# Late half of the first prompt block's index scores in the sample's top-k list, and the index key and head weights in one pass of 72 columns

## The chip, the cores and the metric

The kernel runs on one core of a Trainium2 chip, in one launch. The metric is the device time of that execution in microseconds, the median of several runs. TensorE (PE), VectorE (DVE), ScalarE (ACT), GpSimd (POOL) and SyncE (SP, which issues most DMAs) each run their own instruction stream, in order, and meet only at semaphores.

## The reference

A streaming encoder step of two layers for 256 prompt frames and 32 sample frames of width 1024, all in float32. Each layer is a half-step FFN, a mixer, and a second half-step FFN, each with RMS norms. The mixer's input projection `w_in` has columns for a convolution branch (a, g), attention (q, k, v, 8 heads of 64) and an indexer (8 index queries of 64, one shared index key of 64, 8 head weights). The indexer decides which keys each query may attend to:

```python
logits = jnp.einsum('thd,sd->ths', qi, ki).astype(jnp.float32) * IDX_SCALE
score = jnp.einsum('th,ths->ts', wi.astype(jnp.float32) * IDX_HEAD_SCALE, jax.nn.relu(logits))
admissible = k_chunk[None, :] <= q_chunk[:, None]
score = jnp.where(admissible, score, -jnp.inf)
_, idx = lax.top_k(score, topk)
valid = k_chunk[idx] <= q_chunk[:, None]
```

A chunk has 64 frames, and a query sees the keys of its own chunk and of earlier ones. A prompt query keeps the top 64 of 256 keys; a sample query the top 136 of 544 (512 cached ones and 32 new). The first 64 prompt queries have exactly 64 admissible keys, so they keep all of them; queries 64 to 127 choose 64 of 128, and those from 128 on choose from 192 or 256. Softmax attention over the kept keys, a causal convolution of width 31 with layer norm and swish beside it, and one output projection follow.

## The kernel before

Activations lie transposed, channels in the 128 partitions and the 288 tokens along the row. Every float32 weight is split into a high and a low part: ACT copies it to `whi` (L403), VectorE (L712) or, in the mixers, GpSimd (L1050) subtracts to `wlo`, and three matmuls (L1110 to L1112) multiply wlo by hh, whi by hl and whi by hh. A projection unit is 128 output columns: 24 matmuls. SP streams the weights through two raw slots; a slot's next load waits for the low splits that read it. The order of work is written out by hand for each engine.

The mixer's stages on TensorE: step 0 of the input projection (units 0 to 3, the index queries, `first_step`); then the index key and the head weights, called the tail; then the partner products of the rotation (L1221, one for each of the four index-query tiles and one for kiT) between the units of step 1. Partner k from 2 on waits for rotation k-2 to be done (`rope_done`), since two PSUM banks serve five products. Then come the transposes of head weights and cached keys, the index logits of eight heads, steps 2 to 5 of the projection (in the code `in_step`), the partners of q and k, value transposes, and ten attention rounds (`logits`, `turn`, `values`). `partners(9)` waits until the rotations of q are done.

The tail's weights come in by three DMAs from GpSimd's queue (L1083): the 64 key columns twice, so that the key lands in both halves of the partitions, and the 8 head-weight columns; 136 columns in all. ACT splits the high part (L492), VectorE the low part (L876). TensorE makes two passes of 24 matmuls (L1207 to L1209), one with 128 columns to bank 4 and one with 8 columns to bank 5, and ACT copies them to kiT (L505) and wiT (L507).

VectorE in the mixer: L876; the reciprocal root (L727); cosR and sinR (L879, L880); the rotations (L838 multiplies a tile by cosR, L839 the partner in PSUM by sinR, L843 adds them); the head weights (L884 to L896); then for each head two operations that add a weighted relu'd logit tile to the score tile (L903, L905): 128 columns for prompt queries 0 to 127, 256 for queries 128 to 255. Two memsets of 64 x 64 bar the inadmissible keys (L910, L911), L913 copies the sample's scores (32 rows, 544 columns) behind them, and `top_k` runs. A round of a list is one MAX8 (L864: the eight largest of each row) and one MATCH_REPLACE8 (L866: mark these as taken), each waiting for the one before on the same list. Two lists are interleaved: the sample's with 17 rounds of 32 x 544, and the prompt's with eight rounds of 128 x 128 followed by eight of 128 x 256.

```python
top_k([[(slice(0, DEC), 384, 928, TOPK_S)],
       [(slice(0, P), 0, P, TOPK_P), (slice(0, P), P, 384, TOPK_P)]])
```

After that VectorE scales the conv branch by the inverse root (L922, L923; the first releases ACT's sigmoid, L537, and through it ACT's copies and weight splits of step 4), makes the sample's mask in four copies (L926) and the prompt's in place over 384 columns (L928), multiplies the gate (L933, L934, which release ACT's and its own convolution work), runs 8 of its 83 convolution steps (L946, L950), rotates q, runs 14 more steps, rotates k, and goes on with convolution steps between the attention rounds. GpSimd splits weights (L1050, four operations a step), each released by ACT's high split, and later adds convolution products (L1097).

Of the kernel before, what the change touches and what calls it, by code (L numbers as in the profile page):

```python
# [15 lines left out]
ALU = mybir.AluOpType  # L16
ACT = mybir.ActivationFunctionType

P = 128
D = 1024  # L20
SEQ = 256
DEC = 32
T = SEQ + DEC
# [27 lines left out]
WIDX = 2 * HD + HEADS  # L51
# [38 lines left out]
def build(nc, ins, consts, outs):  # L90
    (y_prompt, y_sample, prompt_k, prompt_v, prompt_ki, prompt_conv,
     sample_k, sample_v, sample_ki, sample_conv) = outs
    with ExitStack() as ctx:
# [5 lines left out]
        def sb(name, shape, dt=F32):  # L99
            size = int(np.prod(shape[1:])) * 4  # L100
            t = nc.alloc_sbuf_tensor_at(name, list(shape), dt, offset=BASE + at[0])
            at[0] += (size + 31) // 32 * 32
            assert at[0] <= SIZE - 64, (name, at[0])
            return t
# [39 lines left out]
        wiT = sb("wiT", [HEADS, T])  # L144
# [6 lines left out]
        score = sb("score", [P, 928])  # L151
# [9 lines left out]
        wtlo = sb("wtlo", [P, KD, WIDX], F32R)  # L161
        rel_at = at[0]
# [227 lines left out]
        def _(act):  # L390
# [97 lines left out]
            def mixer(m, s):  # L488
                u = mix_unit(m)

                act.wait_ge(tail_in, 48 * (m + 1))
# [12 lines left out]
                act.wait_ge(tail_done, 2 * m + 1)  # L504
                act.activation(kiT[:], bank(4), ACT.Copy).then_inc(tail_saved, 1)  # L505
                act.wait_ge(tail_done, 2 * m + 2)
                act.activation(wiT[:], bank(5, slice(0, HEADS)), ACT.Copy).then_inc(tail_saved, 1)  # L507
# [192 lines left out]
        def _(dve):  # L700
# [172 lines left out]
            def mixer(m, s, g, hq_next, g_next):  # L873
# [23 lines left out]
                for h in range(HEADS):  # L897
                    dve.wait_ge(rel_ready, 8 * m + h + 1)
                    for a, b, w0 in ((0, P, 0), (P, 384, 8)):
                        src = relP[:, h % 2, a:b]  # L900
                        w = wrow[:, w0 + h:w0 + h + 1]
                        if h == 0:
                            last = dve.tensor_scalar(score[:, a:b], src, w, None, ALU.mult)  # L903
                        else:
                            last = dve.scalar_tensor_tensor(out=score[:, a:b], in0=src, scalar=w,  # L905
                                                            in1=score[:, a:b], op0=ALU.mult, op1=ALU.add)
                    last.then_inc(rel_used, 1)
                    dve.wait_ge(rel_used, 8 * m + h + 1)

                dve.memset(score[0:CHUNK, CHUNK:P], BARRED)  # L910
# [4 lines left out]
                top_k([[(slice(0, DEC), 384, 928, TOPK_S)],  # L915
                       [(slice(0, P), 0, P, TOPK_P), (slice(0, P), P, 384, TOPK_P)]])
# [11 lines left out]
                link(dve.tensor_scalar(score[:, 0:384], score[:, 0:384], TAKEN, NEG, ALU.not_equal, ALU.mult))  # L928
# [30 lines left out]
                def softmax_max(n):  # L959

                    dve.wait_ge(s_done, 10 * m + n + 1)
                    if n >= 2:
                        dve.wait_ge(pT_done, 10 * m + n - 1)
                    spans = [(0, SKEYS)] if n < 2 else [(0, P), (P, 384)]
                    c = 8 * n
                    for j, (a, b) in enumerate(spans):
                        logits = ps[:, 1024 * (n % 2) + a:1024 * (n % 2) + b]
                        mask = maskS[:] if n < 2 else score[:, a:b]
                        link(dve.tensor_tensor_reduce(prob[:, n % 2, a:b], logits, mask, HD ** -0.5, -3.0e38,  # L969
                                                      ALU.add, ALU.max, stat[:, c + j:c + j + 1]))  # L970
                    k = len(spans)
                    dve.tensor_scalar(stat[:, c + 2:c + 2 + k], stat[:, c:c + k], -1.0, None,
                                      ALU.mult).then_inc(max_ready, 1)
# [49 lines left out]

            dve.memset(ones[:], 1.0)
# [21 lines left out]
        def _(pool):  # L1046
# [29 lines left out]
            for m in range(DEPTH):  # L1076
# [4 lines left out]
                for d, (c0, n) in ((0, (KI_COL, HD)), (HD, (KI_COL, HD)), (2 * HD, (KI_COL + HD, HEADS))):  # L1081
                    with nc.allow_non_contiguous_dma(reason="8 head-weight columns"):
                        pool.dma_start(wtail[:, :, d:d + n], w_in[:, :, c0:c0 + n]).then_inc(tail_in, 16)  # L1083
# [23 lines left out]
        def _(pe):  # L1107
# [91 lines left out]
            def mixer(m, s, hq):  # L1199
# [4 lines left out]
                for b, c0, n in ((4, 0, P), (5, P, HEADS)):  # L1204
                    for k in range(KD):
                        o = bank(b, slice(0, n))
                        pe.matmul(o, wtlo[:, k, c0:c0 + n], hh[:, k, :], start=(k == 0), stop=False)  # L1207
                        pe.matmul(o, wthi[:, k, c0:c0 + n], hl[:, k, :], start=False, stop=False)
                        last = pe.matmul(o, wthi[:, k, c0:c0 + n], hh[:, k, :], start=False, stop=(k == KD - 1))  # L1209
                    last.then_inc(tail_done, 1)  # L1210
# [32 lines left out]
                for tt, (t0, n) in enumerate(TOK):  # L1243
                    pe.transpose(bank(4, slice(0, n), 8 * tt, 8), wiT[:, t0:t0 + n], ident[0:HEADS, 0:HEADS])
                    last = pe.matmul(bank(4, slice(0, n), 24 + tt, 1), rinv[0:1, t0:t0 + n], ones[0:1, 0:1],
                                     start=True, stop=True)
# [297 lines left out]
```

## Time and profile before

| | |
|---|---|
| runs | 1392.57, 1393.87, 1399.64 us; median 1393.87 |
| profiled execution | span 1389.6 us from the first to the last instruction; no own run time is listed for it |
| PE, PEld busy | 1266.4 us (91%), 1202.5 us (87%) |
| DVE busy | 936.1 us (67%), 1555 instructions |
| ACT, POOL busy | 655.4 us (47%), 290.0 us (21%) |
| mean granted TensorE clock | 0.941 |
| mixers | about 242 to 476 us and 920 to 1154 us of the span |

The busy shares are means over the FFNs, where TensorE is full, and the mixers, where it isn't. A matmul's traced duration (about 0.29 us) overlaps its neighbours'; the distance between their starts is what counts. A DVE operation's duration includes the time in which it has been started and is held up.

### The profile page before, as it was taken

Reading aid. Unit: us, or ns where it says so; the run is one execution under the profiler, and the core shown is the slowest. Engines: PE = TensorE matmul, PEld = TensorE weight load, DVE = VectorE, ACT = ScalarE, POOL = GpSimd, SP = SyncE. Lnnn points to the kernel's source line nnn. Section 1 sums busy time; section 2 is a strip of 40 time slices with the busy share of each in tenths; the row PEclk is TensorE's granted clock in tenths of the full one; section 3 lists DMA queues with packets and bytes.
Section 4 is the critical chain, followed back from the end, with each engine's and each line's share of the span. In section 5 each row is a group of like instructions: output and inputs, shape, how many; then the busy total and the mean of one; then the engine's idle time right before and its main releaser. Section 6 shows DMA issues by size and latency. Waiting matters only on the chain.

```text
span 1389.6 us, 24055 instructions
## 1 busy us (share of the span) xinstructions
PE 1266.4 (91%) x9033; PEld 1202.5 (87%) x9033; DVE 936.1 (67%) x1555; ACT 655.4 (47%) x1100; POOL 290.0 (21%) x214
## 2 busy tenths in 40 slices
PE   5999999999367899999989999999966689999998
PEld 4999999889255899999989999987964479999998
DVE  3766644779996676664476665466999957766543
ACT  3544444444365654444455444454335475544432
POOL 3000000546461610000020000035564425000000
PEclk9999999999757999999999999999985599999998
DMA  5454555523200435454535455553340023545451
GB/s 173 141 184 159 164 173 164 161 92 125 87 0 1 161 122 181 151 165 156 165 119 184 154 171 164 164 190 122 106 138 1 0 70 123 173 160 180 144 167 58
DMA packets 179540, 184.63 MB, mean 133 GB/s; under 512 B 6627, under 2 KB 174827, under 8 KB 179470
## 3 DMA queue, kind: packets, MB, share of 16 engines
q1 hardware_dynamic: 178030, 181.93, 40.6%
q0 software_dynamic: 1056, 1.62, 0.5%
q8 instruction: 46, 0.75, 0.2%
q14 instruction: 24, 0.20, 0.0%
q10 hardware_dynamic: 384, 0.13, 0.0%
HBM read 179.73 MB, written 3.93 MB: 132 GB/s over the span
## 4 chain that ended last, share of the span: by engine, by line
PE 68%; DVE 25%; ACT 3%; issue 3%; DMA 0%; DVEq 0%; SPq 0%; ACTq 0%
PE ps L1110 21%; PE ps L1112 20%; PE ps L1111 20%; DVE yc L950 6%; DVE score L866 2%; DVE acc L736 2%; DVE m L864 2%; DVE x L757 2%; DVE hl L722 2%; DVE upd L749 1%; DVE prob L981 1%; DVE prob L969 1%; DVE ropb L839 1%; PE ps L1340 1%; DVE proj L843 1%
## 5 line engine op out<-in xcount | busy, mean ns | idle before, releaser
L1110 PE MATMUL ps<-hh,wlo 128*128 128x288 f32 x1920 | 575.8, 300 | 19.2 <-DVE hl L722 10.1
L1111 PE MATMUL ps<-hl,whi 128*128 128x288 f32 x1920 | 567.6, 296 | 0.0
L1112 PE MATMUL ps<-hh,whi 128*128 128x288 f32 x1920 | 565.8, 295 | 0.0
L712 DVE TENSOR_TENSOR wlo<-raw,whi 128x1024 fp32r<-128x1024 f32 (+1 forms) x269 | 320.5, 1193 | 287.0 <-ACT whi L403 283.7
L403 ACT ACTIVATE whi<-raw 128x1024 fp32r<-128x1024 f32 (+1 forms) x336 | 347.4, 1035 | 236.5 <-PE ps L1112 213.2
L1110 PEld LDWEIGHTS ps<-hh,wlo 128*128 128x128 f32 x1920 | 361.2, 188 | 27.5 <-issue 14.2
L1112 PEld LDWEIGHTS ps<-hh,whi 128*128 128x128 f32 x1920 | 362.7, 189 | 0.0
L1111 PEld LDWEIGHTS ps<-hl,whi 128*128 128x128 f32 x1920 | 361.9, 188 | 0.6
L1050 POOL TENSOR_TENSOR wlo<-raw,whi 128x1024 fp32r<-128x1024 f32 x67 | 166.3, 2499 | 492.1 <-ACT whi L403 492.0
L1110 PE MATMUL ps<-ghi,wlo 128*128 128x288 f32 x704 | 208.4, 296 | 0.0
L1111 PE MATMUL ps<-glo,whi 128*128 128x288 f32 x704 | 207.7, 295 | 0.0
L1112 PE MATMUL ps<-ghi,whi 128*128 128x288 f32 x704 | 207.0, 294 | 0.0
L1112 PEld LDWEIGHTS ps<-ghi,whi 128*128 128x128 f32 x704 | 132.6, 188 | 0.0
L1111 PEld LDWEIGHTS ps<-glo,whi 128*128 128x128 f32 x704 | 132.2, 188 | 0.0
L1110 PEld LDWEIGHTS ps<-ghi,wlo 128*128 128x128 f32 x704 | 131.9, 187 | 0.0
L950 DVE SCALAR_TENSOR_TENSOR yc<-ext,taps,yc 128x318 f32<-128x318 f32 x160 | 116.2, 794 | 0.0
L451 ACT ACTIVATE sil<-sil 128x288 f32<-128x288 f32 x88 | 38.8, 445 | 151.2 <-DVE sil L788 151.2
L1097 POOL TENSOR_TENSOR yc<-yc,prod 128x318 f32<-128x318 f32 x78 | 70.4, 903 | 63.1 <-ACT prod L554 54.2
L1083 POOL DMA_DIRECT2D wtail<-in_w_in x6 | 5.3, 895 | 274.5 <-DVE glo L794 274.5
L736 DVE TENSOR_TENSOR acc<-acc,ysq 128x288 f32<-128x288 f32 x42 | 43.4, 1034 | 27.9 <-ACT ysq L434 26.9
L801 DVE TENSOR_TENSOR gt<-ps,rinv 128x288 f32<-128x288 f32 x88 | 40.0, 455 | 21.2 <-PE ps L1112 21.1
L458 ACT ACTIVATE ghi<-gt 128x288 f32 (+1 forms) x88 | 39.1, 445 | 31.9 <-DVE gt L805 25.5
(202 smaller groups left out, 1186.5 us busy)
## 6 DMA issues: line engine op xcount, KB each, us to landing
raw<-in_ffn_w_up SPq DMA_DIRECT2D x88, 1024.0 KB, 5.1
raw<-in_ffn_w_down SPq DMA_DIRECT2D x32, 1024.0 KB, 5.1
raw<-in_w_in SPq DMA_DIRECT2D x24, 1024.0 KB, 5.2
raw<-in_ffn_w_down SPq DMA_DIRECT2D x16, 768.0 KB, 4.5
raw<-in_w_out SPq DMA_DIRECT2D x8, 1024.0 KB, 5.1
kc<-in_cache_k SPq DMA_DIRECT2D x2, 1024.0 KB, 8.1
vc<-in_cache_v SPq DMA_DIRECT2D x2, 1024.0 KB, 8.3
xrow<-in_x_prompt SPq DMA_DIRECT2D x1, 1024.0 KB, 5.4
```

What stands on the lines that cost most here:

```text
L403: act.activation(whi[:, split_slot, 0:n, :], raw[:, raw_slot, 0:n, half * P:(half + 1) * P], ACT.Copy).then_inc(hi_ready, 1)
L451: act.activation(sil[:, j * T:(j + 1) * T], sil[:, j * T:(j + 1) * T], ACT.Silu).then_inc(silu_ready, 1)
L458: act.activation(ghi[:, bass.ds((2 * i + j) * T, T)], gt[:, j * T:(j + 1) * T], ACT.Copy).then_inc(ghi_ready, 1)
L712: dve.tensor_tensor(wlo[:, split_slot, 0:n, :], raw[:, raw_slot, 0:n, cols], whi[:, split_slot, 0:n, :].bitcast(F32), ALU.subtract).then_i ...
L736: dve.tensor_tensor(acc[:], acc[:], ysq[:, slot * T:(slot + 1) * T], ALU.add).then_inc(acc_ready, 1)
L801: dve.tensor_tensor(gt[:, j * T:(j + 1) * T], bank(b0[2 + j]), rinv[:], ALU.mult).then_inc(up_ready, 1)
L950: ins_ = dve.scalar_tensor_tensor(out=yc[:, ct, :], in0=src, scalar=w, in1=yc[:, ct, :], op0=ALU.mult, op1=ALU.add)
L1050: pool.tensor_tensor(wlo[:, split_slot, :, :], raw[:, raw_slot, :, cols], whi[:, split_slot, :, :].bitcast(F32), ALU.subtract).then_inc(lo ...
L1097: pool.tensor_tensor(dst, dst, prod[:, n % 3, :], ALU.add).then_inc(pconv_ready, 1)
L1110: pe.matmul(out, wlo[:, slot, k, :], hi, start=start, stop=False)
L1111: pe.matmul(out, whi[:, slot, k, :], lo, start=False, stop=False)
L1112: return pe.matmul(out, whi[:, slot, k, :], hi, start=False, stop=stop)
```

## The change

The head weights and the key are computed in one pass. The tail's weights are loaded once as 72 neighbouring columns by one DMA, split once (576 elements a row instead of 1,088), and 24 matmuls of 72 columns give bank 4 rows 0 to 63 (key) and 64 to 71 (head weights). ACT copies the key twice, to both halves of kiT, and the weights to rows 64 to 71 of wiT; the transposes read from there.

The scores of queries 64 to 127 go to rows 64 to 127 of the sample's area (columns 384 to 511), so that one list covers both: eight rounds over 128 rows and 544 columns, then nine over the sample's 32 rows. The rest of that area is barred by two larger memsets. Queries 0 to 63 take no part, and their mask is constant: a new tile `seen`, set up once, holds 0 for the 64 admissible keys and the mask value for the others; its rows 64 to 127 are written each layer. The prompt's other list has only the eight rounds of 256 columns. The prompt mask (L928) becomes two operations.

```diff
-WIDX = 2 * HD + HEADS
+WIDX = HD + HEADS
...
-                act.wait_ge(tail_done, 2 * m + 1)
-                act.activation(kiT[:], bank(4), ACT.Copy).then_inc(tail_saved, 1)
-                act.wait_ge(tail_done, 2 * m + 2)
-                act.activation(wiT[:], bank(5, slice(0, HEADS)), ACT.Copy).then_inc(tail_saved, 1)
+                act.wait_ge(tail_done, m + 1)
+                for half in range(2):
+                    last = act.activation(kiT[half * HD:(half + 1) * HD, :], bank(4, slice(0, HD)), ACT.Copy)
+                last.then_inc(tail_saved, 1)
+                act.activation(wiT[HD:WIDX, :], bank(4, slice(HD, WIDX)), ACT.Copy).then_inc(tail_saved, 1)
...
-                    for a, b, w0 in ((0, P, 0), (P, 384, 8)):
-                        src = relP[:, h % 2, a:b]
-                        w = wrow[:, w0 + h:w0 + h + 1]
+                    late = slice(CHUNK, P)
+                    for rows, a, b, o, w0 in ((late, 0, P, 384, 0), (slice(0, P), P, 384, P, 8)):
+                        src = relP[rows, h % 2, a:b]
+                        w = wrow[rows, w0 + h:w0 + h + 1]
+                        dst = score[rows, o:o + b - a]
...
-                dve.memset(score[0:CHUNK, CHUNK:P], BARRED)
+                dve.memset(score[late, 384 + P:928], BARRED)
+                dve.memset(score[DEC:CHUNK, 384:928], BARRED)
                 dve.memset(score[0:CHUNK, P + 3 * CHUNK:P + 4 * CHUNK], BARRED)
...
-                top_k([[(slice(0, DEC), 384, 928, TOPK_S)],
-                       [(slice(0, P), 0, P, TOPK_P), (slice(0, P), P, 384, TOPK_P)]])
+                top_k([[(slice(0, P), 384, 928, TOPK_P), (slice(0, DEC), 384, 928, TOPK_S - TOPK_P)],
+                       [(slice(0, P), P, 384, TOPK_P)]])
...
-                link(dve.tensor_scalar(score[:, 0:384], score[:, 0:384], TAKEN, NEG, ALU.not_equal, ALU.mult))
+                dve.tensor_scalar(seen[late, :], score[late, 384:384 + P], TAKEN, NEG, ALU.not_equal, ALU.mult)
+                link(dve.tensor_scalar(score[:, P:384], score[:, P:384], TAKEN, NEG, ALU.not_equal, ALU.mult))
...
-                        mask = maskS[:] if n < 2 else score[:, a:b]
+                        mask = maskS[:] if n < 2 else score[:, a:b] if a else seen[:]
...
+            dve.memset(seen[0:CHUNK, 0:CHUNK], 0.0)
+            dve.memset(seen[0:CHUNK, CHUNK:P], NEG)
...
-                for d, (c0, n) in ((0, (KI_COL, HD)), (HD, (KI_COL, HD)), (2 * HD, (KI_COL + HD, HEADS))):
-                    with nc.allow_non_contiguous_dma(reason="8 head-weight columns"):
-                        pool.dma_start(wtail[:, :, d:d + n], w_in[:, :, c0:c0 + n]).then_inc(tail_in, 16)
+                pool.dma_start(wtail[:], w_in[:, :, KI_COL:KI_COL + WIDX]).then_inc(tail_in, 16)
...
-                for b, c0, n in ((4, 0, P), (5, P, HEADS)):
-                    for k in range(KD):
-                        o = bank(b, slice(0, n))
-                        pe.matmul(o, wtlo[:, k, c0:c0 + n], hh[:, k, :], start=(k == 0), stop=False)
-                        pe.matmul(o, wthi[:, k, c0:c0 + n], hl[:, k, :], start=False, stop=False)
-                        last = pe.matmul(o, wthi[:, k, c0:c0 + n], hh[:, k, :], start=False, stop=(k == KD - 1))
-                    last.then_inc(tail_done, 1)
+                for k in range(KD):
+                    o = bank(4, slice(0, WIDX))
+                    pe.matmul(o, wtlo[:, k, :], hh[:, k, :], start=(k == 0), stop=False)
+                    pe.matmul(o, wthi[:, k, :], hl[:, k, :], start=False, stop=False)
+                    last = pe.matmul(o, wthi[:, k, :], hh[:, k, :], start=False, stop=(k == KD - 1))
+                last.then_inc(tail_done, 1)
```

## Rows read from the trace of the kernel before

**Rows 1.** The page, part 4: shares of the chain that ended last, by line
```profile
PE ps L1110 21%; PE ps L1112 20%; PE ps L1111 20%; DVE yc L950 6%; DVE score L866 2%; DVE acc L736 2%; DVE m L864 2%; DVE x L757 2%; DVE hl L722 2%; DVE upd L749 1%; DVE prob L981 1%; DVE prob L969 1%; DVE ropb L839 1%; PE ps L1340 1%; DVE proj L843 1%
```

**Rows 2.** Busy time by stretch: us, DVE busy, PEclk, DMA share, GB/s
```profile
298.70:331.00 32.30, 32.20 (x101) 1.00 0.42 130
331.00:363.00 32.00, 31.87 (x30) 0.84 0.40 132
```

**Rows 3.** Timeline of DVE, top-k of the first layer: start us, us, engine, line, operation
```profile
298.76 0.91 DVE L864 MAX8 m<-score 32x8 f32<-32x544 f32 x2
...
312.96 1.03 DVE L864 MAX8 m<-score 32x8 f32<-32x544 f32 x2
...
329.29 0.70 DVE L864 MAX8 m<-score 32x8 f32<-32x544 f32 x1
...
330.84 1.36 DVE L922 TENSOR_TENSOR proj<-proj,rinv 128x1152 f32<-128x1152 f32 x1
```

**Rows 4.** Timeline of DVE, the two clears ahead of the top-k
```profile
297.96 0.11 DVE L910 MEMSET score<- 64x64 f32 x1
298.04 0.11 DVE L911 MEMSET score<- 64x64 f32 x1
```

**Rows 5.** Groups of DVE instructions by line and form: busy us, mean ns
```profile
L731 DVE MEMSET acc<- 128x288 f32 x6 | 1.8, 298 | 0.1
```

**Rows 6.** Timeline of DVE, masks, gates, convolution and rotation of q, first layer
```profile
333.38 1.77 DVE L926 TENSOR_SCALAR maskS<-score 32x544 f32<-32x544 f32 x4
335.17 2.43 DVE L928 TENSOR_SCALAR score<-score 128x384 f32<-128x384 f32 x1
...
340.86 2.49 DVE L934 TENSOR_TENSOR ext<-proj 128x128 f32<-128x128 f32 x1
...
346.43 10.82 DVE L950 SCALAR_TENSOR_TENSOR yc<-ext,taps,yc 128x318 f32<-128x318 f32 x5
...
358.20 0.45 DVE L839 TENSOR_TENSOR ropb<-ps,sinR 128x288 f32<-128x288 f32 x1
```

**Rows 7.** Timeline of POOL in the first mixer, with idle time before and its releaser
```profile
265.12 2.59 POOL L1050 TENSOR_TENSOR wlo<-raw,whi 128x1024 fp32r<-128x1024 f32 x1
...
272.29 2.48 POOL L1050 TENSOR_TENSOR wlo<-raw,whi 128x1024 fp32r<-128x1024 f32 x1 [4.59 <-ACT whi L403]
...
334.72 10.89 POOL L1050 TENSOR_TENSOR wlo<-raw,whi 128x1024 fp32r<-128x1024 f32 x4 [8.44 <-ACT whi L403]
346.81 10.09 POOL L1050 TENSOR_TENSOR wlo<-raw,whi 128x1024 fp32r<-128x1024 f32 x4 [1.20 <-ACT whi L403]
356.86 2.94 POOL L1097 TENSOR_TENSOR yc<-yc,prod 128x318 f32<-128x318 f32 x3
```

**Rows 8.** Timeline of PE around the tail's two passes and the partner products
```profile
260.19 0.29 PE L1207 MATMUL ps<-hh,wtlo 128*128 128x288 f32 x1
...
266.50 1.13 PE L1221 MATMUL ps<-proj,swap 128*128 128x288 f32 x4
...
270.66 0.65 PE L1221 MATMUL ps<-proj,swap 128*128 128x288 f32 x2
...
272.68 0.72 PE L1221 MATMUL ps<-proj,swap 128*128 128x288 f32 x2 [1.37 <-DVE proj L843]
```

**Rows 9.** Timeline of DVE, sinR and rotation of the index queries, first layer
```profile
262.82 2.65 DVE L880 TENSOR_TENSOR sinR<-sinT,rinv 128x288 f32<-128x288 f32 x1
267.25 0.77 DVE L838 TENSOR_TENSOR ropa<-proj,cosR 128x288 f32<-128x288 f32 x1 [1.78 <-PE ps L1221]
...
272.09 0.45 DVE L843 TENSOR_TENSOR proj<-ropa,ropb 128x288 f32<-128x288 f32 x1
273.44 1.65 DVE L838 TENSOR_TENSOR ropa<-proj,cosR 128x288 f32<-128x288 f32 x1 [0.91 <-PE ps L1221]
```

**Rows 10.** The page, part 5: ACT's high splits: busy us, mean ns, idle before
```profile
L403 ACT ACTIVATE whi<-raw 128x1024 fp32r<-128x1024 f32 (+1 forms) x336 | 347.4, 1035 | 236.5 <-PE ps L1112 213.2
```

**Rows 11.** Busy time by stretch: us, PE busy, PEclk, DMA share, GB/s
```profile
353.00:354.00 1.00, 0.00 (x0) 0.50 0.75 212
```

More of the change, by code:

```diff
@@ L143, in build @@
         kiT = sb("kiT", [P, T])
-        wiT = sb("wiT", [HEADS, T])
+        wiT = sb("wiT", [WIDX, T])
         wrow = sb("wrow", [P, 3 * HEADS])
@@ L150, in build @@
         stack = sb("stack", [P, DEC])
-        score = sb("score", [P, 928])
+        score = sb("score", [P, P + 2 * P + SKEYS])
+        seen = sb("seen", [P, P])
         m8 = sb("m8", [P, 16])
@@ L161, in build @@
         wtlo = sb("wtlo", [P, KD, WIDX], F32R)
+        at[0] = g_at + 4 * SKEYS * 4
         rel_at = at[0]
@@ L489, in mixer @@
                 u = mix_unit(m)
-                act.wait_ge(tail_in, 48 * (m + 1))
+                act.wait_ge(tail_in, 16 * (m + 1))
                 act.activation(wthi[:], wtail[:], ACT.Copy).then_inc(tail_hi, 1)
@@ L898, in mixer @@
                     dve.wait_ge(rel_ready, 8 * m + h + 1)
-                    for a, b, w0 in ((0, P, 0), (P, 384, 8)):
-                        src = relP[:, h % 2, a:b]
-                        w = wrow[:, w0 + h:w0 + h + 1]
+                    late = slice(CHUNK, P)
[3 more added lines that the diff above has]
+                        dst = score[rows, o:o + b - a]
                         if h == 0:
-                            last = dve.tensor_scalar(score[:, a:b], src, w, None, ALU.mult)
+                            last = dve.tensor_scalar(dst, src, w, None, ALU.mult)
                         else:
-                            last = dve.scalar_tensor_tensor(out=score[:, a:b], in0=src, scalar=w,
-                                                            in1=score[:, a:b], op0=ALU.mult, op1=ALU.add)
+                            last = dve.scalar_tensor_tensor(out=dst, in0=src, scalar=w, in1=dst, op0=ALU.mult, op1=ALU.add)
                     last.then_inc(rel_used, 1)
                     dve.wait_ge(rel_used, 8 * m + h + 1)
-                dve.memset(score[0:CHUNK, CHUNK:P], BARRED)
+                dve.memset(score[late, 384 + P:928], BARRED)
+                dve.memset(score[DEC:CHUNK, 384:928], BARRED)
                 dve.memset(score[0:CHUNK, P + 3 * CHUNK:P + 4 * CHUNK], BARRED)
@@ L1243, in mixer @@
                 for tt, (t0, n) in enumerate(TOK):
-                    pe.transpose(bank(4, slice(0, n), 8 * tt, 8), wiT[:, t0:t0 + n], ident[0:HEADS, 0:HEADS])
-                    last = pe.matmul(bank(4, slice(0, n), 24 + tt, 1), rinv[0:1, t0:t0 + n], ones[0:1, 0:1],
+                    pe.transpose(bank(4, slice(0, n), 8 * tt, 8), wiT[HD:WIDX, t0:t0 + n], ident[HD:WIDX, HD:WIDX])
+                    last = pe.matmul(bank(4, slice(0, n), 24 + tt, 1), rinv[HD:HD + 1, t0:t0 + n], ones[HD:HD + 1, 0:1],
                                      start=True, stop=True)
```

## The prediction

> **What bounds the kernel now.** I read the chain of work that ended last first, then the busy time by stretch, then the timelines of one mixer engine by engine. By its shares the chain is TensorE work for two thirds and VectorE work for a quarter, and the VectorE lines in it are those of the mixer: the convolution (L950) and the top-k pair L864 and L866 [rows 1]. TensorE's part is the FFNs, which the change leaves alone. In the stretches the reader is to see that VectorE is busy for 32.20 of 32.30 us while the top-k runs and for 31.87 of 32 us after it [rows 2]. TensorE is full in the first of these too, but with projection units that nobody waits for until VectorE has done masks, gating, eight convolution steps and the query rotations. So from the first MAX8 on, a microsecond of VectorE is a microsecond of the layer. Ahead of the top-k the order of PE, ACT, VectorE and GpSimd together sets the pace, and the shortened weight pass sits there. Both layers show the same pattern (the second 678 us later), so I work out one and double it.
>
> **Part 1, the top-k list.** Before, eight rounds treat the sample's 544 columns beside 128 columns, the next eight beside 256, and the 17th stands alone. The first eight run from 298.76 to 312.96, 1.775 us each; the next eight from 312.96 to 329.29, 2.04 each; the lone one from 329.29 to 330.84, 1.55 [rows 3]. It is 1.55 and not the two operations' bare time, because each waits for the end of the one before, with no other list to fill the gap. After, the first prompt block's late half rides in the 544-column operations (taken to cost the same over 128 rows as over 32: 128 more columns in all 128 rows lengthen a pair of MAX8 by 0.12 us, 0.9 ns a column, close to the rate of the single one of 544 columns in 32 rows, 0.70 us), the 256-column list fills eight rounds, and nine are left alone: 8 x 2.04 + 9 x 1.55 = 30.3 us against 32.1. **Gain 1.8 us per layer.** Seen from the other side: eight rounds of 1.775 become eight lone ones of 1.55. Bounds: a gain of 3.1 if a lone round cost only what the 544 columns add to a pair (about 1.4), and none if the list over 128 rows were slower by 0.2 a round.
>
> **Part 2, the added clearing.** The two 64-column memsets run at 297.96 and 298.04 and cost about 0.1 us together; a 288-column one takes 298 ns [rows 5] and a 64-column one 0.11 us, so 0.83 ns a column above some 60. The new ones of 416 and 544 columns take 0.40 and 0.51 us, on the path because the copy of the sample's scores stands behind them. The three start in different groups of rows, and so does the copy. The two old ones overlap by 0.03 us [rows 4]; four mask operations that write to four different groups of 32 rows take 1.77 us, 0.44 each, with nothing overlapping [rows 6]. I take no overlap, and 0.08 for the last accumulation pair of L905, whose halves now start in different rows: **loss 0.98 us**, bounds 0.7 and 1.1. [...]
>
> **Part 3, the mask in two operations.** Here VectorE and GpSimd alternate. The 384-column mask L928 takes 2.43 us, the 128-column gate L934 2.49, and five convolution steps 10.82 [rows 6], all while GpSimd runs four weight splits in 10.89 and four in 10.09 us [rows 7]: one such VectorE operation gets through per GpSimd operation. Now the mask is two operations, so one more turn is needed. Before, L928, the two gates and the first convolution step get the four turns; after, both masks and both gates do, and the gate L934 ends at about 346.0 instead of 343.35. But the first convolution step then runs free, so VectorE itself is behind by one short operation, 0.45 us. The second group of splits follows L934 through ACT (343.35 to 346.81 now, 3.5 us) and so moves 2.5 us later. It then meets the rotations of q, of which those that read PSUM are not held up (L839 takes 0.45 us [rows 6] inside three GpSimd additions [rows 7]), instead of five convolution steps in a row. That gives back nothing to 1.7 us, by how many of the four turns fall on a PSUM reader's neighbour. Net between a gain of 1.3 and a loss of 0.45; I take **a gain of 0.5 us**, near the middle. The rigid alternation might also charge a whole turn, 2.5 us: that is a rival.
>
> **Part 4, one pass of 72 columns.** The two passes, 24 matmuls of 128 and 24 of 8 columns, start at 260.19 and the partner products behind them at 266.50 [rows 8]: 131 ns a matmul, so one pass of 72 columns takes 3.15 us and TensorE is free 3.15 sooner. What does it reach? The first rotation product L838 waits for VectorE's sinR, which ends at 265.47 [rows 9], and then for GpSimd's fourth split, from 265.12 to 267.71 [rows 7]. It ends at 268.02 before, 0.31 behind that split, and would after. Unit 4 of the projection (266.50 to 270.66 with its products) ends at 267.5 instead; through ACT the next GpSimd split starts at 269.16 instead of 272.29. TensorE, 3.1 us early, must wait for the first rotation (269.5) before the third product, which is ready at 270.4. Its L838 now lands inside that split, ends 0.31 us behind it at 271.95, and the second rotation's sum L843 ends at 272.7, against 272.54 now [rows 9]. The fourth product, which waits for it (272.68 now, idle 1.37 before it [rows 8]), starts 0.15 us later, and everything behind with it; the 1.65 us that L838 takes at 273.44 now falls to 0.45 and helps nobody, as PE is in a unit then. **Gain nothing, loss 0.15 us**: the 3.1 us turn into two waits of about 2 and 2.7 us ahead of the third and fourth product. Bounds: a gain of 3.1 if the waits follow TensorE, a loss of 0.3. The high split of 72 columns has 576 elements a row against 1,088, and by the weight splits' 1035 ns for 1,024 [rows 10] that saves ACT 0.5 us; it could move GpSimd's four splits by as much. Behind it on ACT stand the copies of the projection units that TensorE is just closing, so I take nothing. GpSimd issues one DMA instead of three when the FFN's up half ends, and the whole down half of the FFN hides it: nothing; uncovered, two issues less would be a gain, not a loss. The second kiT copy costs ACT 0.4 us in a pause. The fifth product, which needs kiT, comes only after the unit that starts at about 273.5.
>
> **Sum:** -1.8 + 0.98 - 0.5 + 0.15 = -1.2 us per layer, -2.3 us in all. The profiled execution has a span of 1389.6 us, 4.3 under the median of the three runs, 1393.87; the same difference from the median gives **1391.6**.
>
> **Rivals.**
> A whole turn is lost (slower than before): place, the gate L934; point, whether conv steps and rotations can use the time that ACT and GpSimd arrive later. If they can't, 2.5 us stand in place of the gain of 0.5: +1.8 per layer, 1397.5. For it: the strict alternation and that ACT's convolution products hang on L934. Against it: VectorE is never idle there, and the same eight splits are to be passed either way. Chance 0.12.
> The TensorE pass counts in full: -1.2 - 3.3 = -4.5 per layer, 1384.9. For it: PE is busy there; a split that started after L838 instead of before would let it through. Against it: the 1.2 us by which the split would start ahead of L838 (269.16 against 270.4). Chance 0.10.
> [...] Between 267.5 and 272.8 TensorE would do only one product. If the next unit of 3.2 us ran at half speed it would add up to 3.2 us: +2.0 per layer, 1398. [...] Chance 0.08.
> The change brings nothing on the path (alone rounds dearer or memsets dearer by 1 us): 1394. Chance 0.10.
> The forecast, 0.60.
>
> **Numbers.** About 0.5%, 7 us, is what a measurement of this kernel can tell from no change. Only the second rival, with a gain in part 3, lies beyond it; a tenth for faster. A fall of the clock together with a lost turn would be beyond on the other side; 0.03. The range reaches up to the lost turn and the fallen clock, 1398.5, and down over the full gain of part 3 and a part of TensorE's, 1388; the full TensorE gain and the ends of the others, some 2 in 10, are left out.
>
> **What would show it.** L864 and L866: no operations of 128 columns (16 of each per layer now), nine lone rounds of 1.55 us, the top-k 1.8 us shorter. Two memsets of 0.40 and 0.51. L934 ends some 15.2 us after the first operation behind the top-k instead of 12.5, and the rotation of q ends no later than before. L1221 waits twice, 2 and 2.7 us; its third L838 takes about 1.6 us. The forecast is wrong if the start of the top-k moves by more than 0.5 us towards the FFN's end, or if the granted clock leaves 1.00 between 267 and 284.

## The result and the profile after

The changed kernel takes 1399.16 us (median of ten runs, 1397.06 to 1401.16), against 1393.94 for the kernel before on the same chips. The ratio is 1.0039, with a 95% interval of 1.0027 to 1.0051: slower by some 5 us, where I forecast 2.3 us less. The page of its profiled execution:

```profile
span 1399.0 us, 23915 instructions
...
PE 1277.4 (91%) x8985; PEld 1211.8 (87%) x8985; DVE 937.0 (67%) x1513; ACT 655.4 (47%) x1102; POOL 289.7 (21%) x210
```

Its span is 1399.0; the whole program has 140 instructions fewer. The second line shows that TensorE's busy time has grown by 11 us, although 48 matmuls are gone: less work at a lower clock. The mean granted clock is 0.929 instead of 0.941. The two profiled executions lie further apart (9.4 us) than the medians (5.2): the one of the kernel before is among its fastest, the one of the changed kernel among its slowest. Over its ten executions the changed kernel's mean granted clock is 0.929 to 0.936, against 0.934 to 0.946 in the recorded ones of the kernel before.

To see where, I cut each mixer at the starts of VectorE operations that both kernels have (times in us, first layer / second layer):

| stretch on VectorE | before | after | expected change | measured change |
|---|---|---|---|---|
| reciprocal root to first MAX8 | 39.42 / 39.43 | 43.66 / 43.29 | +1.1 | +4.2 / +3.9 |
| top-k | 32.08 / 32.08 | 30.35 / 30.35 | -1.8 | -1.7 |
| top-k end to gate's last operation end | 12.51 / 12.52 | 14.81 / 14.81 | +2.7 | +2.3 |
| from there to the 14 convolution steps behind the rotation of q | 19.26 / 19.28 | 16.77 / 16.76 | -3.2 | -2.5 |
| from there over the rotation of k to the first attention maximum | 13.62 / 13.62 | 13.62 / 15.22 | 0 | 0 / +1.6 |
| attention rounds, to the norm of the convolution | 67.11 / 67.88 | 69.36 / 66.69 | 0 | +2.3 / -1.2 |

The first line holds the surprise. The first four add up to 2.3 and 1.9 us more per layer, 4.2 of the 5 us or so that the time grew by. The last two vary within one kernel, so no kernel below is judged by them. In the fifth line the trace shows where: the six convolution steps that end the stretch take 2.85 or 4.45 us, and three additions that GpSimd does beside them take 4.47 or 2.77:

```profile
377.04 2.85 DVE L956 SCALAR_TENSOR_TENSOR yc<-ext,taps,yc 128x318 f32<-128x318 f32 x6
...
1060.14 4.45 DVE L956 SCALAR_TENSOR_TENSOR yc<-ext,taps,yc 128x318 f32<-128x318 f32 x6
```

In all 24 mixers of the twelve profiled executions the slow steps go with the quick additions and the quick steps with the slow ones; what decides between the two isn't shown. TensorE in the first line's stretch, as its timeline has it (L1226 are the partner products):

```profile
264.63 1.13 PE L1226 MATMUL ps<-proj,swap 128*128 128x288 f32 x4
...
270.90 0.72 PE L1226 MATMUL ps<-proj,swap 128*128 128x288 f32 x2 [1.95 <-DVE proj L846]
...
274.15 1.30 PE L1226 MATMUL ps<-proj,swap 128*128 128x288 f32 x2 [2.52 <-DVE proj L846]
...
280.70 0.65 PE L1226 MATMUL ps<-kiT,swap 128*128 128x288 f32 x2
```

These are to be read against [rows 8]. The products start at 264.63, and behind the first projection unit TensorE now waits 1.95 us, does one product, and waits 2.52 us: the two waits that part 4 worked out as 2 and 2.7. But the next product takes 1.30 us instead of 0.72, and the unit behind it lasts until 280.70, 6 us. From the start of the fourth product to the start of the fifth it is 6.55 us, where it was 3.74 (272.68 to 276.42). By busy time and granted clock, one microsecond a line:

```profile
272.00:273.00 1.00, 0.00 (x0) 1.00 1.09 388
273.00:274.00 1.00, 0.00 (x0) 0.73 0.68 233
274.00:275.00 1.00, 0.85 (x3) 0.50 0.00 0
...
279.00:280.00 1.00, 1.00 (x6) 0.50 0.00 0
...
281.00:282.00 1.00, 1.00 (x9) 1.00 0.00 0
```

The granted clock goes from 1.00 to 0.50 in the second wait and stays there through most of the unit, until 280.3. In brackets stands how many matmuls run in the microsecond, also those that began before it: 6 from 279 to 280, against 9 or 10 from 281 on. Their starts lie 0.24 us apart in the slow part of the unit and 0.13 behind it. VectorE in the same stretch, against [rows 9]:

```profile
264.09 2.62 DVE L883 TENSOR_TENSOR sinR<-sinT,rinv 128x288 f32<-128x288 f32 x1
266.75 2.54 DVE L841 TENSOR_TENSOR ropa<-proj,cosR 128x288 f32<-128x288 f32 x1
...
271.66 1.60 DVE L841 TENSOR_TENSOR ropa<-proj,cosR 128x288 f32<-128x288 f32 x1 [0.91 <-PE ps L1226]
...
273.56 0.44 DVE L846 TENSOR_TENSOR proj<-ropa,ropb 128x288 f32<-128x288 f32 x1
...
281.38 0.46 DVE L841 TENSOR_TENSOR ropa<-kiT,cosR 128x288 f32<-128x288 f32 x1 [4.71 <-PE ps L1226]
```

L841 is the first rotation operation of a product, L846 the sum. The first takes 2.54 us, from 266.75 to 269.29, beside GpSimd's fourth split, which ends at 268.97; the third, at 271.66, takes 1.60 beside this one, where the second takes 0.44:

```profile
270.48 2.47 POOL L1058 TENSOR_TENSOR wlo<-raw,whi 128x1024 fp32r<-128x1024 f32 x1 [1.51 <-ACT whi L405]
...
338.49 10.78 POOL L1058 TENSOR_TENSOR wlo<-raw,whi 128x1024 fp32r<-128x1024 f32 x4 [7.93 <-ACT whi L405]
352.78 10.31 POOL L1058 TENSOR_TENSOR wlo<-raw,whi 128x1024 fp32r<-128x1024 f32 x4 [3.51 <-ACT whi L405]
```

The split at 270.48 ends at 272.95 and the held operation at 273.26, 0.31 behind it, so the second rotation is no earlier than before, counted from the reciprocal root, but 0.2 us later. The line at 281.38 shows what follows: VectorE has no product for 4.7 us, since TensorE is in its slow unit. The other two lines are the two groups of four splits, the second now 3.51 us after the first ends, where it was 1.20 [rows 7]. VectorE from the last accumulation on:

```profile
301.43 0.85 DVE L910 SCALAR_TENSOR_TENSOR score<-relP,wrow,score 64x128 f32<-64x128 f32 x2 [1.62 <-ACT relP L530]
302.43 0.41 DVE L914 MEMSET score<- 64x416 f32 x1
302.98 0.51 DVE L915 MEMSET score<- 32x544 f32 x1
...
304.26 1.05 DVE L867 MAX8 m<-score 128x8 f32<-128x544 f32 x2
...
320.60 0.70 DVE L867 MAX8 m<-score 32x8 f32<-32x544 f32 x1
...
322.14 0.72 DVE L867 MAX8 m<-score 32x8 f32<-32x544 f32 x1
...
334.61 1.36 DVE L927 TENSOR_TENSOR proj<-proj,rinv 128x1152 f32<-128x1152 f32 x1
...
338.94 2.31 DVE L933 TENSOR_SCALAR seen<-score 64x128 f32<-64x128 f32 x1
341.26 2.40 DVE L934 TENSOR_SCALAR score<-score 128x256 f32<-128x256 f32 x1
...
346.94 2.48 DVE L940 TENSOR_TENSOR ext<-proj 128x128 f32<-128x128 f32 x1
...
353.57 2.29 DVE L841 TENSOR_TENSOR ropa<-proj,cosR 128x288 f32<-128x288 f32 x1
355.78 0.44 DVE L842 TENSOR_TENSOR ropb<-ps,sinR 128x288 f32<-128x288 f32 x1
```

The two large clears take 0.41 and 0.51 us. They don't overlap: 0.15 us lies ahead of the first (0.06 ahead of the small clear that stood there), 0.14 between the two, and 0.05 ahead of the third. With the accumulation pair, now 0.85 us, the stretch from that pair's start to the first MAX8 is 2.83 us, against 1.61 before (297.15 to 298.76). A lone round of the top-k takes 1.54 us (320.60 to 322.14). The masks at 338.94 and 341.26 and the gates behind them each take one GpSimd turn, and in the rotation L841 and L846 are held (2.29 us at 353.57) while L842 isn't (0.44 at 355.78).

### The profile page after: what moved, and what is told of

The parts are those of the page before. It is cut to its first block, busy times and chain, and to the rows that moved or that the text cites. A ratio compares the mean times of both kernels' runs of the same rounds, so it can differ in the third digit from the quotient of the medians.

```text
span 1399.0 us, 23915 instructions
## 1 busy us (share of the span) xinstructions
PE 1277.4 (91%) x8985; PEld 1211.8 (87%) x8985; DVE 937.0 (67%) x1513; ACT 655.4 (47%) x1102; POOL 289.7 (21%) x210
## 4 chain that ended last, share of the span: by engine, by line
PE 66%; DVE 25%; ACT 4%; issue 3%; DMA 1%; POOL 1%; DVEq 0%; SPq 0%; ACTq 0%
PE ps L1116 21%; PE ps L1118 20%; PE ps L1117 20%; DVE yc L956 6%; DVE score L869 2%; DVE m L867 2%; DVE x L760 2%; DVE hl L725 2%; DVE upd L752 1%; DVE proj L846 1%; DVE acc L739 1%; DVE prob L987 1%; DVE ropa L841 1%; POOL wlo L1058 1%; DVE prob L975 1%
## 5 line engine op out<-in xcount | busy, mean ns | idle before, releaser
L956 DVE SCALAR_TENSOR_TENSOR yc<-ext,taps,yc 128x318 f32<-128x318 f32 x160 | 100.6, 699 | 0.0
L1103 POOL TENSOR_TENSOR yc<-yc,prod 128x318 f32<-128x318 f32 x78 | 74.1, 949 | 58.8 <-ACT prod L557 49.6
L1089 POOL DMA_DIRECT2D wtail<-in_w_in x2 | 1.8, 916 | 275.4 <-DVE glo L797 275.4
```

What stands on the lines that cost most here:

```text
L956: ins_ = dve.scalar_tensor_tensor(out=yc[:, ct, :], in0=src, scalar=w, in1=yc[:, ct, :], op0=ALU.mult, op1=ALU.add)
L1103: pool.tensor_tensor(dst, dst, prod[:, n % 3, :], ALU.add).then_inc(pconv_ready, 1)
```

## Experiments

There are two theories. **Clock:** the single pass empties TensorE in two waits that VectorE and GpSimd set, the granted clock falls, and the slow unit costs about 3 us per layer. **Turns:** the two mask operations and the larger clears cost more than they save. Ratios are to runs of the kernel before on the same chip, with 95% intervals.

### The single pass alone

The kernel before with the tail's part of the change: one DMA, one pass, the copies of kiT and wiT.

```diff
-WIDX = 2 * HD + HEADS
+WIDX = HD + HEADS
...
+                for k in range(KD):
+                    o = bank(4, slice(0, WIDX))
```

> Only the pass of 72 columns and its loads, splits and copies; the top-k lists stay as before. Clock theory (the 3.1 us that TensorE saves become two waits of about 2 and 2.5 us, the granted clock falls to 0.50 in them and the next projection unit takes about 6 us instead of 3.2): the start of the top-k moves some 3.1 us later per layer, the kernel is 6 us slower than before, about 1.0045. Rival (the slowdown comes from the two mask operations and the larger clears): about 1.0002, since only 0.15 us per layer is lost here.

Measured: 1398.96 us, ratio 1.0042 (1.0027 to 1.0058). From the root to the top-k it takes 41.61 and 42.43 us against 39.42 and 39.43. The whole slowdown is in this half of the change. The clock falls here too, in the first layer already behind the single product between the waits:

```profile
269.00:270.00 1.00, 0.72 (x2) 0.92 0.94 322
270.00:271.00 1.00, 0.00 (x0) 0.50 1.09 384
...
274.00:275.00 1.00, 1.00 (x6) 0.50 0.00 0
...
277.00:278.00 1.00, 1.00 (x10) 1.00 0.00 0
```

It falls at the end of that product, 0.8 us behind its start, where in the changed kernel it was 2.6 us. The cost differs by layer, 2.2 and 3.0 us, with the moment at which the clock falls and comes back: from the fourth product to the fifth it takes 5.73 us in the first layer and 6.55 in the second, against 3.74.

### The shared list alone

```diff
-                top_k([[(slice(0, DEC), 384, 928, TOPK_S)],
-                       [(slice(0, P), 0, P, TOPK_P), (slice(0, P), P, 384, TOPK_P)]])
+                top_k([[(slice(0, P), 384, 928, TOPK_P), (slice(0, DEC), 384, 928, TOPK_S - TOPK_P)],
+                       [(slice(0, P), P, 384, TOPK_P)]])
```

> Only the shared top-k list, its clears and the two mask operations; the weight passes stay as before. Clock theory: TensorE has no new waits, so the granted clock stays 1.00 until the top-k; 1.75 us saved in the rounds, about 1.0 lost in clears and accumulation, 0.2 gained behind: 1 us less per layer, ratio 0.9986. Rival (a whole turn between VectorE and GpSimd is lost on the way): 1.8 us more per layer, ratio 1.0026.

Measured: 1392.37 us, ratio 0.9991 (0.9981 to 1.0001), where 0.9986 was expected; that of the turns theory, 1.0026, lies far outside the interval. Turns falls. The stretches are 40.66 us to the top-k (+1.24), 30.36 for it (-1.72), and 14.82 + 16.77 for masks to rotation (-0.18), in both layers: 0.66 us less per layer, 1.3 in all, and 1.3 was measured. TensorE has its one old wait of 1.4 us.

### TensorE filled again

The changed kernel, with 24 matmuls of 8 columns behind the single pass; their results are not used.

```diff
                 last.then_inc(tail_done, 1)
+                for n in range(24):
+                    pe.matmul(bank(5, slice(0, HEADS)), wthi[:, n % KD, 0:HEADS], hh[:, n % KD, :], start=True, stop=True)
```

> The changed kernel with 24 matmuls of 8 columns added behind the pass of 72 columns, results unused, so that TensorE is as busy as before there. Clock theory: the clock stays 1.00, the unit behind the waits takes 3.2 us again, and the time falls from 1399 to about 1392, ratio 0.9986, although 24 matmuls are added. Rival (the time was lost in lists, clears or masks): no change from the changed kernel or slower, 1.004.

Measured: 1393.73 us, ratio 0.9999 (0.9989 to 1.0009). Work without a use makes the changed kernel some 5 us faster. Its TensorE timeline:

```profile
263.52 3.34 PE L1217 MATMUL ps<-hh,wthi 128*8 128x288 f32 x24
266.70 0.65 PE L1228 MATMUL ps<-proj,swap 128*128 128x288 f32 x2
...
272.88 0.72 PE L1228 MATMUL ps<-proj,swap 128*128 128x288 f32 x2 [1.38 <-DVE proj L846]
```

The fill stands where the second pass stood, the waits are the 1.4 us of before, the granted clock is 1.00 from 264 to 285, and from the root to the top-k it takes 40.67 and 40.70 us, within 0.04 us of the kernel with the shared list alone. The total is 1.7 us above the expectation and 1.4 above that kernel's, whose interval overlaps; the stretches show nothing that it would come from. The fourth product starts 13.4 us behind the reciprocal root, against 13.6 in the changed kernel, so the 24 matmuls cost nothing; from there to the fifth it takes 3.75 us instead of 6.55. That is the slow clock's 2.8 of the 3.0 us in the first layer, and 2.4 of 2.6 in the second.

### Only the first wait filled

```diff
                 in_unit(1, 0)
+                for n in range(12):
+                    pe.matmul(bank(5, slice(0, HEADS)), wthi[:, n % KD, 0:HEADS], hh[:, n % KD, :], start=True, stop=True)
                 partner(2)
```

> The changed kernel with 12 matmuls of 8 columns (1.6 us, results unused) in the first of TensorE's two new waits only; the second wait of about 2.5 us stays empty. If one wait of 2.5 us behind a full stretch leaves the clock at 1.00, as the 1.4 us one of before did, the result is that of the fully filled kernel, ratio 1.000; if that wait alone lets it fall, the unit behind it stays slow, ratio 1.003 to 1.004.

Measured: 1396.87 us, ratio 1.0019 (1.0011 to 1.0028), between the two. The timeline of the first layer shows the first wait nearly gone and the second as it was:

```profile
267.80 1.76 PE L1241 MATMUL ps<-hh,wthi 128*8 128x288 f32 x12
...
269.88 0.72 PE L1226 MATMUL ps<-proj,swap 128*128 128x288 f32 x2 [0.32 <-DVE proj L846]
...
273.13 0.72 PE L1226 MATMUL ps<-proj,swap 128*128 128x288 f32 x2 [2.52 <-DVE proj L846]
```

By busy time and granted clock in the same run:

```profile
272.00:273.00 1.00, 0.00 (x0) 1.00 0.56 196
...
274.00:275.00 1.00, 1.00 (x8) 0.71 0.00 0
275.00:276.00 1.00, 1.00 (x6) 0.50 0.00 0
...
278.00:279.00 1.00, 1.00 (x8) 1.00 0.00 0
```

The clock falls after this one wait too, but later, behind the start of the unit, and for a shorter time: 42.35 and 42.87 us to the top-k, 1.7 and 2.2 more than with the full fill. In the second layer the wait itself is longer, 3.19 us, since the last operation of the rotation is held beside a GpSimd split too (L846 takes 2.27 us instead of 0.44); some 0.7 of its 2.2 us are that. So a wait of 2.5 us, with only 0.32 us idle in front of the product ahead of it, is enough here. One of 1.4 us left 1.00 in all eight mixers that have it (the kernel before, the two with the shared list alone, and the one with the full fill).

### The clears moved

The changed kernel with its two large clears ahead of VectorE's wait for the head weights.

```diff
+                dve.memset(score[CHUNK:P, 384 + P:928], BARRED)
+                dve.memset(score[DEC:CHUNK, 384:928], BARRED)
                 dve.wait_ge(wi_T, m + 1)
...
-                dve.memset(score[late, 384 + P:928], BARRED)
-                dve.memset(score[DEC:CHUNK, 384:928], BARRED)
```

> The changed kernel with the two large clears (416 and 544 columns) moved ahead of VectorE's wait for the head weights, where it is idle for 3.5 us. If the clears cost what their durations say where they stand, 0.95 us per layer comes back: 1397.2, ratio 1.0024; if they were covered there or something else is late, the ratio stays at 1.0039. The clock fall ahead of them stays as in the changed kernel.

Measured: 1397.71 us, ratio 1.0026 (1.0014 to 1.0039), as expected: the clears stood on the path and there was idle time for them elsewhere. From the root to the top-k it takes 42.16 and 41.78 us, 1.5 each below the changed kernel; 1.2 of it is what the later runs confirm (below), the other 0.3 the slow unit, which isn't equally long in every execution (6.23 and 5.86 us from the fourth product to the fifth, against 6.55 and 6.17).

### Accumulation over all rows

The kernel with the shared list alone, its first accumulation over rows 0 to 127 instead of 64 to 127; what it writes in rows 0 to 63 is overwritten.

```diff
-                    for rows, a, b, o, w0 in ((late, 0, P, 384, 0), (slice(0, P), P, 384, P, 8)):
+                    for rows, a, b, o, w0 in ((slice(0, P), 0, P, 384, 0), (slice(0, P), P, 384, P, 8)):
```

> The kernel with only the shared list, whose accumulation for the first prompt block runs over all 128 rows again instead of rows 64 to 127 (rows 0 to 63 of it are overwritten by a clear and by the sample's scores). If the different start rows cost the pairs their overlap, a pair of L910 falls from 0.85 to 0.75 us, and the stretch from the root to the top-k from 40.66 to about 40.4 us; if not, both stay.

This kernel was run once; the time of 1394.93 us says nothing at this size, the timeline does:

```profile
297.23 0.75 DVE L908 SCALAR_TENSOR_TENSOR score<-relP,wrow,score 128x128 f32<-128x128 f32 x2 [1.82 <-ACT relP L528]
298.12 0.41 DVE L912 MEMSET score<- 64x416 f32 x1
298.68 0.51 DVE L913 MEMSET score<- 32x544 f32 x1
```

The pair takes 0.75 us instead of 0.85, and the stretch to the top-k 40.55 and 40.54 instead of 40.66: the effect is there, 0.1 us on the path where 0.26 was expected. The clears still start in other rows and still stand 0.15 us apart.

### The third product in the free bank

The single pass leaves PSUM bank 5 free, so the third product needn't wait for the first rotation, and the fourth and fifth move one unit back.

```diff
-                    if k >= 2:
-                        pe.wait_ge(rope_done, 13 * m + k - 1)
-                    pe.matmul(bank(6 + k % 2), swap[:], src, start=True, stop=True).then_inc(rope_mm, 1)
+                    if k >= 3:
+                        pe.wait_ge(rope_done, 13 * m + k - 2)
+                    pe.matmul(bank((6, 7, 5, 6, 7)[k]), swap[:], src, start=True, stop=True).then_inc(rope_mm, 1)
...
                 partner(1)
-                in_unit(1, 0)
                 partner(2)
-                partner(3)
+                in_unit(1, 0)
                 in_unit(1, 1)
-                partner(4)
+                partner(3)
                 in_unit(1, 2)
+                partner(4)
                 in_unit(1, 3)
```

VectorE reads the same banks, and the key transposes into bank 5 wait for the third rotation.

> The changed kernel; the third partner product goes to bank 5, which the single pass has left free, right behind the second, and the fourth and fifth stand one projection unit later, so that TensorE has no wait there. Clock theory: the granted clock stays 1.00, units of 3.2 us, and now the 3.1 us saved by the single pass count: from the root to the top-k about 38 us instead of 43.5, 4 to 5.5 us less per layer than the changed kernel; total about 1389 to 1390, ratio 0.9970. Rival (the unit behind the waits is slow for another reason, such as its weights being late): little change, ratio 1.003.

Measured: 1385.65 us, ratio 0.9945 (0.9932 to 0.9957), a larger gain than expected. Its TensorE timeline has no wait at any partner product, and the first three products (six matmuls) stand together:

```profile
262.74 1.62 PE L1226 MATMUL ps<-proj,swap 128*128 128x288 f32 x6
...
270.57 0.65 PE L1226 MATMUL ps<-proj,swap 128*128 128x288 f32 x2
...
274.24 0.65 PE L1226 MATMUL ps<-kiT,swap 128*128 128x288 f32 x2
```

The granted clock is 1.00 throughout, and from the root to the top-k it takes 35.90 and 35.87 us: 7.8 and 7.4 less than the changed kernel, and 4.8 less than with the fill: the 3.2 us of the pass, the 1.4 us that TensorE waited even before, and 0.2. Against the kernel before the stretches up to the rotation of q are 5.4 us shorter per layer, 10.9 in all, of which 7.7 show in the ratio. In the profiled execution 1.6 of the rest lie in the second layer's convolution steps ahead of the attention, and 0.5 and 0.8 in the attention rounds.

### The same with TensorE filled

> The kernel with the third product in bank 5 and its later order (1385.65 us, TensorE without a wait there), with the 24 matmuls of 8 columns put back behind the single pass, results unused. In the changed kernel the same 24 matmuls made it faster by 5. If TensorE's own work now sets the start of the top-k, they cost their 3.1 us per layer here: ratio 0.9945 + 0.0045 = 0.999. If the gain of the new order came only from the clock that no longer falls, they cost nothing or little: ratio 0.995 to 0.996.

The edit is the fill of above. Measured: 1388.35 us, ratio 0.9978 (0.9969 to 0.9987); the stretch to the top-k is 39.06 and 39.09 us, 3.2 more than without the fill. So here the same 24 matmuls cost their full time:

```profile
262.76 3.34 PE L1217 MATMUL ps<-hh,wthi 128*8 128x288 f32 x24
265.94 1.62 PE L1228 MATMUL ps<-proj,swap 128*128 128x288 f32 x6
```

They stand between the pass and the six partner products with nothing idle around them. The total differs by 0.0033 instead of the 0.0046 that two times 3.2 us make; the rest lies within the intervals.

### The fastest versions

> The same with the two large clears moved ahead of VectorE's wait for the head weights: 0.9 us per layer less again, about 1387.5, ratio 0.9955. It should be faster than both kernels. If the clears then delay the head weights, because VectorE is no longer idle there, the ratio is that of the run without the move.

The third product in bank 5 and the early clears together: 1383.80 us, ratio 0.9926 (0.9913 to 0.9939). The stretch to the top-k is 34.68 and 34.69 us: the clears give 1.2 us per layer, although in the run without the move VectorE waits only 0.26 us for the head weights: behind them the first operation on `wdiag` takes 0.24 us instead of 1.00 in the first layer, and the wait for ACT's relu is 0.31 instead of 0.52, which takes up the delay. It beats both kernels, the changed one by about 15 us.

> The fastest kernel so far (third product in bank 5, early clears), with the first prompt block's accumulation over all 128 rows again, so that neighbouring operations start in the same row, and one clear of 32 rows and 128 columns behind it for the rows that this touches. By the pairs (0.75 us against 0.85) it gains 0.1 to 0.2 us per layer and pays as much for the clear: ratio 0.9926 as before, within the noise; a change of more than 0.001 would mean that the start rows cost more than the trace shows.

1380.49 us, ratio 0.9919 (0.9906 to 0.9932); the stretch is 34.80 and 34.82, 0.12 longer: the added clear costs slightly more than the pairs give back, and the difference in the total is within the noise.

## Why the prediction was wrong

**The step that failed** is in part 4: "**Gain nothing, loss 0.15 us**: the 3.1 us turn into two waits of about 2 and 2.7 us ahead of the third and fourth product." The waits came, 1.95 and 2.52 us, for the reason given, the GpSimd split that holds the rotation, and the 0.15 us by which the second rotation was to be later were 0.2. But I priced the waits as time in which nothing happens and took the unit behind them at full clock. In its place the runs show a clock at 0.50 and 2.0 to 2.8 us more for the fourth product and that unit, with the 0.2 a loss of 2.2 to 3.0 us per layer: +0.0042 for the pass alone, all of it undone, within the intervals, by useless matmuls in place of the waits. The sign that I had named for this, a granted clock that leaves 1.00 between 267 and 284, came. The fall of the clock stood among the rivals, with this place, as a unit at half speed and up to 3.2 us, at a chance of 0.08; its time of 1398 is within 1.2 us of what came. So the mechanism had been seen, and was put at nothing in the sum; the only row behind it was one from a long pause. The trace of the kernel before held better evidence than the pause of 12 us from 350.5 on that I took [rows 11]. In that pause the granted clock was at 0.88 already from 352 to 353, as the mean of that microsecond. These are TensorE's busy time and granted clock at the end of the first FFN, behind 12 matmuls of one column and around a wait of 0.8 us:

```profile
239.00:240.00 1.00, 0.41 (x4) 1.00 1.08 382
240.00:241.00 1.00, 0.81 (x4) 0.56 0.21 63
241.00:242.00 1.00, 1.00 (x6) 0.50 0.00 0
...
243.00:244.00 1.00, 1.00 (x7) 0.74 0.51 57
```

The clock falls there with gaps far shorter than 12 us, and these lines were missing from the argument. It isn't so every time: in four of the twelve profiled executions it stays at 1.00 in this place of the first layer.

**Part 1**, the rounds: -1.8 expected, -1.72 found. A lone round takes 1.55 us as worked out; MAX8 and MATCH_REPLACE8 over 128 rows and 544 columns take 722 and 713 ns against 715 and 697 over 32 rows.

**Part 2**, the clears and the pair: +0.98 expected, +1.24 found. Their durations (0.405 and 0.512 us) and the 0.1 us of the pair were right; the term that was short is the distances ahead of the clears. They come to 0.28 us more than before (0.15 instead of 0.06, then 0.14 and 0.05), and 0.08 goes off for the small clear that is gone. For the 0.08 us of the pair no row of before stood; the runs show 0.85 us for a pair of different start rows, over 64 and 128 rows, and 0.75 for one of the same, over 128 rows both. Whether the clears' distances come from their start rows or from their size isn't shown: the third clear starts in other rows too and stands only 0.05 us behind.

**Part 3**, two masks: the gate ends 14.8 us behind the start of the first operation after the top-k (15.2 expected), so the turn is lost there. Behind it the eight convolution steps, ahead of GpSimd's second group, take 3.4 us instead of 13.8, and the rotation of q, beside that group, 13.4 instead of 5.4: it gives the turn back, as L842 is not held (0.44 us beside 2.29 for L841). Net -0.2 us instead of -0.5: right in its mechanism, short by 0.3. The rival of a lost turn is refuted by the run with the list alone, 0.9991 where it needed 1.0026.

**The other free terms** were free: with the fill, ACT's second copy and GpSimd's single DMA are still there, and the stretch is that of the shared list alone to 0.04 us.

**The range**, 1388.0 to 1398.5, ended 0.7 us below the median found.

## What to carry to other kernels

Taking work off TensorE can cost time when it then waits for other engines: if the wait lets the granted clock fall, the matmuls behind it take nearly twice as long (0.24 us instead of 0.13 from start to start here), and the kernel is slower with less work. Before you shorten a TensorE stage, find what it will wait for; if that wait can't be moved, the removed matmuls had been useful as a fill, and if it can (here a third PSUM bank and a later place for two small products), the same edit turns from a loss of 0.4% into a part of a gain of 0.7%. Small clears and constants belong where their engine waits, not behind the last input (1.2 us per layer here).

## What the runs showed of the hardware that I had not expected

A wait of 2.5 us, with 0.32 us idle shortly ahead of it, let TensorE's granted clock fall from 1.00 to 0.50 (the run with one wait filled), while a wait of 1.4 us in the same place left it at 1.00 in eight mixers out of eight. Waits of 1.9 and 2.5 us with one product of 0.72 us between them let it fall in six out of six. Where it fell and came back differed between the two layers of one execution, and so did its cost, 2.2 and 3.0 us. Ahead of the two large clears VectorE left 0.15 and 0.14 us, ahead of a small one 0.05 or 0.06; no run separates their size from their start rows. Six convolution steps of VectorE beside three additions of GpSimd took either 2.85 us, with 4.47 for the additions, or 4.45 with 2.77, and both were seen within one execution: one engine's gain was the other's loss.
